# One merged stage for prompt attention and paged sample attention in a forgetting-attention layer

## The reference, cut to what matters

```python
# prompt: blocks of 128 queries, c_k = cumulative sum of log forget values
sc = einsum('bqhd,bkhd->bhqk', qi, k) * scale + ci[..., None] - c_k[:, :, None, :]
sc = where(pi[:, None] >= pos[None, :], sc, NEG_INF)
out = einsum('bhqk,bkhd->bqhd', softmax(sc), v)

# sample: 2048 past keys of a sequence lie in 16 pages of 128 keys of a pool
k_past, v_past, lf_past = (pool[page_table] ... for k, v and log forget values)
r_past = cumsum(lf_past, axis=1, reverse=True) - lf_past
s_past = einsum('bqhd,bkhd->bhqk', q, k_past) * scale + cq + r_past
s_new  = einsum('bqhd,bkhd->bhqk', q, k) * scale + cq - cq', causal
p = softmax(concatenate([s_past, s_new], axis=-1))
out = einsum(p past, v_past) + einsum(p new, v)
```

## Time and profile before

| what | value |
|---|---|
| runs of the kernel | 2106.39 and 2113.93 us, median 2110.16 us |
| the profiled execution | span 2106.6 us |
| PE busy | 1840.3 us (87%) |
| PEld busy | 1610.9 us (76%) |
| DVE busy | 982.8 us (47%) |
| ACT busy | 537.1 us (25%) |
| POOL busy | 172.2 us (8%) |
| forget sums, prompt and sample stages of layer 1 | from 1106.40 to 1595.12 us |

### The profile page before, as it was taken

The page is one execution under the profiler, slowest core; times in us unless marked ns, Lnnn a source line. Parts: engine busy times, 40 slices in busy tenths (PEclk is TensorE's granted clock), DMA queues, the critical chain, the costliest instruction groups (busy, mean ns, idle before and its releaser), DMA issues.

```text
span 2106.6 us, 36927 instructions
## 1 busy us (share of the span) xinstructions
PE 1840.3 (87%) x13959; PEld 1610.9 (76%) x13959; DVE 982.8 (47%) x1689; ACT 537.1 (25%) x880; POOL 172.2 (8%) x332
## 2 busy tenths in 40 slices
PE   5999466899999999799766788888878899999998
PEld 4876345799999999699634456566557799999997
DVE  5396965533333222776457864444433533333222
ACT  3210233322222111433222323222312322222110
POOL 1010000000000000444100001122220000000000
PEclk9999867999999999999878769999988999999999
DMA  3210121222222322223421027788873222223221
GB/s 113 63 38 30 40 76 61 59 80 85 84 80 81 95 83 71 64 75 87 159 91 61 1 84 276 283 290 312 302 231 97 60 80 86 83 80 91 83 82 58
DMA packets 231243, 224.30 MB, mean 106 GB/s; under 512 B 12114, under 2 KB 199588, under 8 KB 231162
## 3 DMA queue, kind: packets, MB, share of 16 engines
q1 hardware_dynamic: 210736, 150.49, 23.1%
q0 software_dynamic: 19008, 69.43, 9.5%
q10 hardware_dynamic: 1418, 3.29, 0.5%
HBM read 215.37 MB, written 7.80 MB: 106 GB/s over the span
## 4 chain that ended last, share of the span: by engine, by line
PE 74%; DVE 14%; ACT 4%; DMA 3%; issue 3%; POOLq 0%; ACTq 0%; DVEq 0%; POOL 0%
PE ps L1335 54%; PE ps L1708 5%; PE ps L1544 3%; DMA vring<-in_cache_fox_v_dram 3%; PE ps L1720 2%; PE ps L1317 2%; PE ps L1746 2%; DVE tmp L382 1%; DVE stat L468 1%; PE ps L1725 1%; ACT prob L1046 1%; DVE prob L459 1%; DVE prob L494 1%; DVE yc L687 1%; DVE aL L386 1%
## 5 line engine op out<-in xcount | busy, mean ns | idle before, releaser
L1335 PE MATMUL ps<-aH,wH 128*128 128x288 f32 x2224 | 487.5, 301 | 51.8 <-DVE aL L386 34.6
L1335 PE MATMUL ps<-aL,wH 128*128 128x288 f32 x2224 | 480.3, 298 | 0.0
L1335 PE MATMUL ps<-aH,wL 128*128 128x288 f32 x2224 | 479.9, 298 | 0.0
L1335 PEld LDWEIGHTS ps<-aH,wH 128*128 128x128 f32 x2224 | 361.9, 191 | 61.2 <-issue 39.1
L363 DVE TENSOR_TENSOR wL<-raw,wH 128x1024 fp32r<-128x1024 f32 (+1 forms) x179 | 232.0, 1296 | 337.0 <-ACT wH L985 333.9
L1335 PEld LDWEIGHTS ps<-aL,wH 128*128 128x128 f32 x2224 | 362.3, 191 | 0.0
L1335 PEld LDWEIGHTS ps<-aH,wL 128*128 128x128 f32 x2224 | 362.2, 191 | 0.0
L985 ACT ACTIVATE wH<-raw 128x1024 fp32r<-128x1024 f32 (+1 forms) x179 | 198.8, 1111 | 386.6 <-PE ps L1335 358.1
L1335 PE MATMUL ps<-gH,wH 128*128 128x288 f32 x704 | 151.1, 296 | 4.8 <-DVE gL L605 4.8
L1335 PE MATMUL ps<-gH,wL 128*128 128x288 f32 x704 | 151.1, 295 | 0.0
L1335 PE MATMUL ps<-gL,wH 128*128 128x288 f32 x704 | 150.9, 295 | 0.0
(11 more groups left out here) (295 smaller groups left out, 1982.8 us busy)
## 6 DMA issues: line engine op xcount, KB each, us to landing
kring<-in_cache_fox_k_dram SPq DMA_DIRECT2D x128, 384.0 KB, 4.7
vring<-in_cache_fox_v_dram POOLq DMA_DIRECT2D x128, 384.0 KB, 5.2
raw<-in_w_gate_up_dram SPq DMA_DIRECT2D x88, 512.0 KB, 3.8
raw<-in_w_down_dram SPq DMA_DIRECT2D x32, 704.0 KB, 4.6
raw<-in_fox_w_in_dram SPq DMA_DIRECT2D x21, 512.0 KB, 3.9
raw<-in_w_out_dram SPq DMA_DIRECT2D x16, 512.0 KB, 3.8
raw<-in_conv_w_in_dram SPq DMA_DIRECT2D x14, 512.0 KB, 3.9
raw<-in_w_mem_kv_dram SPq DMA_DIRECT2D x8, 512.0 KB, 3.4
```

Of the source, the lines that this page charges most:

```text
L1335: mm = nc.tensor.matmul(ps[:, 2 * slot + h, 0:HT], weights[:, w], a[:, k0 + k, h * HT:(h + 1) * HT], start=(first and k == 0 and weights i ...
```

## The change

The forget sums move beside the memory attention: `forget(i)` runs in its unit i. The prompt and sample stages become one. It has SLOTS = 32 slots, SPB = 4 for each sequence, of SPG = 4 pages (512 keys), and four more slots for the values of the last sequence. The loops over b are gone; every slot is written out. The rings have three chunks.

*Prompt.* `fox_step` cuts the prompt into STEPS = 30 steps of up to 512 key columns of one head (two heads or blocks together where blocks are short), five for two heads. Step i has its maximum, exponential and scaling in slot i, its transposes and values in slot i + 1; its scores stand at the end of slot i - 1.

*Keys.* `keys_T` transposes keys on DVE in 32 by 32 blocks from SBUF to SBUF, two instructions of 128 x 1536 in a slot, into `KT[s % 2]`. The queries are laid out to match: `qr` is built by 16 ACT copies ahead of `memory_kv(1)`, and `spread(b)` makes `qx4` and `qx` from it and from `qkT` by eight ACT copies.

*Scores.* `slot_scores` makes 96 products of tiles with 32 rows and 32 columns (128 keys), and 48 that add `rx` (32 keys). The scores of a sequence stay in PSUM banks 0 to 3 until its exponential has read them; the copies to `S` go.

*Values.* At the head of a slot PE multiplies both chunks of values that fall to the slot, for the sequence before, ahead of the slot's scores. Bank 4 holds their sum, bank 5 the scores of a prompt step, and banks 6 and 7 are taken in turn (`turn_ready`, `turn_free`) by probability transposes, prompt values, new scores, outputs and broadcast forget sums (`c_keys`).

*Other engines.* ACT makes the copies from PSUM that DVE made (probabilities, `ncb`, the scaled output). POOL copies `rx` for four pages (`forget_rows`) into a single buffer, for which it waits until the scores before have been made (`sc_done`); the copy for slot 5 + j stands in its program ahead of the load of chunk 2j + 3. SP waits for `kt_done` where it waited for `kt_ready`.

In the diff below DVE's part comes first, then ACT's, PE's, SP's and POOL's.

```diff
-    RING = 4
+    RING = 3
+    SLOTS = NB * NCH // 2
+    SPB = SLOTS // NB
+    SPG = 2 * CPG
...
+    STEPS = 5 * HP
...
+    def fox_step(i):
+        two, k = divmod(i, 5)
+        e, hp = two % 2, two - two % 2
+        parts = ([(0, 3, 0, SEQ)], [(1, 3, 0, SEQ)], [(0, 0, 0, P), (0, 2, P, 3 * P)], [(1, 0, 0, P), (1, 2, P, 3 * P)],
+                 [(0, 1, 0, 2 * P), (1, 1, 2 * P, 2 * P)])[k]
+        return k, e, [(n, hp + n, t, col, keys) for n, t, col, keys in parts]
...
+            def forget(i):
+                if i == 0:
+                    dve.wait_ge(lf_in, 16 * NB * NP)
+                    nc.vector.tensor_reduce(lftot[:], lfrow[:].rearrange("n (k h) -> n h k", h=NH), AX_X, ALU.add).then_inc(lftot_done, 1)
+                if i < 2 * (NH // 4):
+                    g = i % (NH // 4)
+                    bank = group()
+                    nc.vector.tensor_copy((lfT if i < NH // 4 else rtok)[:, 4 * g:4 * g + 4, :].rearrange("p h n -> p (h n)"),
+                                          bank).then_inc(tr_free, 1)
+            attend(u, MEM_UNITS, mb1, len(MEM_UNITS), forget)
...
+            def keys_T(s):
+                if s >= 2:
+                    dve.wait_ge(sc_done, s - 1)
+                for x in range(2):
+                    n = 2 * s + x
+                    dve.wait_ge(k_in[n % RING], 32 * (n // RING + 1))
+                    nc.vector.transpose(KT[s % 2][:, CPG * x:CPG * x + CPG, :].rearrange("p a n -> p (a n)"),
+                                        kring[n % RING][:].rearrange("p a n -> p (a n)")).then_inc(kt_done, 1)
...
+            def step_top(i):
...
+                if k == 0:
+                    for n in range(2):
+                        wait_taken(dve, ("ncb", i // 5, n))
+                dve.wait_ge(f_scores, i + 1)
+                for n, hp, t, col, keys in parts:
+                    last = nc.vector.scalar_tensor_tensor(out=pr[:, col:col + keys], in0=ps[:, 5, col:col + keys],
+                                                          scalar=ctok[:, t, 2 * hp + e:2 * hp + e + 1], in1=ncb[:, n, 0:keys],
+                                                          op0=ALU.add, op1=ALU.add)
+                link(last)
+                if k < 2:
...
+                for x, (n, hp, t, col, keys) in enumerate(parts):
+                    last = nc.vector.tensor_reduce(st[:, x:x + 1], pr[:, col:col + keys], AX_X, ALU.max, negate=True)
+                last.then_inc(f_max, 1)
...
+            def sample_top(b):
...
+                link(nc.vector.tensor_reduce(stat[0:ROWS, 55:56], S[:, NPAST:NPAST + NS], AX_X, ALU.max, negate=True))
+                dve.wait_ge(sc_done, SPB * (b + 1))
+                link(nc.vector.tensor_reduce(stat[0:ROWS, 54:55], ps[0:ROWS, 0:4, :].rearrange("p a n -> p (a n)"), AX_X, ALU.max, negate=True))
+                link(nc.vector.scalar_tensor_tensor(out=stat[0:ROWS, 56:57], in0=stat[0:ROWS, 54:55], scalar=stat[0:ROWS, 55:56],
...
+            for s in range(SLOTS + SPB):
+                b, cc = divmod(s, SPB)
+                if cc == 0 and b:
+                    sample_top(b - 1)
+                    if s <= STEPS:
+                        step_lo(s - 1)
+                if s < STEPS:
+                    step_top(s)
+                if s + 1 < SLOTS:
+                    keys_T(s + 1)
+                if s < STEPS:
+                    step_sums(s)
+                if cc == 0 and b:
+                    sample_sum(b - 1)
+                elif 1 <= s <= STEPS:
+                    step_lo(s - 1)
...
+            act.wait_ge(hn_done, Z + 1 + HP)
+            act.wait_ge(mL_done, KD)
+            for e in range(2):
+                for c in range(2):
+                    r = slice(DH * e + DQ * c, DH * e + DQ * c + DQ)
+                    for a in range(4):
+                        last = nc.scalar.activation(qr[DQ * a:DQ * a + DQ].rearrange("p (g e) c n -> p g e c n", e=2)[:, :, e, c, :],
+                                                    qkT[r, 0:HP, SEQ:T], ACT.Copy)
...
+            def spread(b):
+                if b:
+                    act.wait_ge(sc_done, SPB * b)
+                    wait_turn(act, ("new", b - 1))
+                for m in range(4):
...
+            def sample_exp(b):
+                act.wait_ge(smax_done, b + 1)
+                nc.scalar.activation(S[:, 0:NPAST].rearrange("p (g a i) -> p a g i", a=4, i=DQ),
+                                     ps[0:ROWS, 0:4, :].rearrange("p a (g i) -> p a g i", i=DQ), ACT.Exp, bias=stat[0:ROWS, 56:57],
+                                     accum_out=stat[0:ROWS, 57:58])
...
+            for s in range(SLOTS + SPB):
+                b, cc = divmod(s, SPB)
+                if 1 <= s <= STEPS:
+                    step_probT(s - 1)
+                if cc == 0 and b:
+                    if b >= 2:
+                        sample_scale(b - 2)
+                    if b < NB:
+                        spread(b)
+                    if s <= STEPS:
+                        step_hi(s - 1)
+                    sample_exp(b - 1)
+                if s < STEPS:
+                    step_exp(s)
+                if cc == 1 and b >= 2:
+                    sample_hi(b - 2)
+                if not (cc == 0 and b) and 1 <= s <= STEPS:
+                    step_hi(s - 1)
+                if s < STEPS:
+                    step_scale(s)
+                if (s + 1) % 5 == 0 and s + 1 < STEPS:
...
+            def step_scores(i):
+                k, e, parts = fox_step(i)
+                if i:
+                    pe.wait_ge(f_max, i)
+                r = slice(DH * e, DH * e + DH)
+                for n, hp, t, col, keys in parts:
+                    mm = nc.tensor.matmul(ps[:, 5, col:col + keys], qkT[r, hp, t * P:(t + 1) * P], qkT[r, HP + hp, 0:keys], start=True, stop=True)
+                mm.then_inc(f_scores, 1)
...
+            def slot_scores(s):
+                b, cc = divmod(s, SPB)
+                pe.wait_ge(kt_done, 2 * s + 2)
+                if cc == 0:
+                    pe.wait_ge(qx_done, b + 1)
+                    if b:
+                        pe.wait_ge(sexp_done, b)
+                k4 = KT[s % 2]
+                def out(a, j):
+                    return ps[QR * j:QR * j + QR, a, cc * P:(cc + 1) * P]
+                for m in range(4):
+                    for c in range(2):
+                        for a in range(4):
+                            for j in range(3):
+                                blk, r = 2 * (4 * j + m) + c, slice(DQ * a, DQ * a + DQ)
+                                nc.tensor.matmul(out(a, j).rearrange("p (g i) -> p g i", g=SPG), qx4[r, blk, :], k4[r, :, blk * DQ:blk * DQ + DQ],
+                                                 start=(m == 0 and c == 0), stop=False, skip_group_check=True, tile_position=(DQ * a, QR * j))
+                pe.wait_ge(rx_done, s + 1)
+                for g in range(SPG):
+                    for a in range(4):
+                        for j in range(3):
+                            r = slice(DQ * a, DQ * a + DQ)
+                            mm = nc.tensor.matmul(out(a, j)[:, g * DQ:(g + 1) * DQ], rx[r, g, 4 * j:4 * j + 4, :].rearrange("p h q -> p (h q)"),
+                                                  ident[r, DQ * a:DQ * a + DQ], start=False, stop=(g == SPG - 1), skip_group_check=True,
+                                                  tile_position=(DQ * a, QR * j))
+                mm.then_inc(sc_done, 1)
...
+            def values(b, c):
+                n = NCH * b + c
+                pe.wait_ge(v_in[n % RING], 32 * (n // RING + 1))
                 if c == 0:
...
+            c_keys(0)
+            step_scores(0)
+            for s in range(SLOTS + SPB):
+                b, cc = divmod(s, SPB)
+                step = 1 <= s <= STEPS
+                if step:
+                    step_probT(s - 1)
+                if cc == 0 and b:
+                    if step:
+                        step_values(s - 1)
+                    sample_probT(b - 1)
+                if b:
+                    values(b - 1, 2 * cc)
+                    values(b - 1, 2 * cc + 1)
+                if s < SLOTS:
+                    slot_scores(s)
+                    if cc == SPB - 1:
+                        new_scores(b)
+                if cc == 1 and b >= 2:
+                    sample_out(b - 2)
+                if not (cc == 0 and b) and step:
+                    step_values(s - 1)
+                if (s + 1) % 5 == 0 and s + 1 < STEPS:
+                    c_keys((s + 1) // 5)
+                if s + 1 < STEPS:
+                    step_scores(s + 1)
...
+                which = [sp.value_load(pages[0:1, CPG * n + pp:CPG * n + pp + 1], min_val=0, max_val=N_PHYS - 1) for pp in range(CPG)]
+                if n >= RING:
+                    sp.wait_ge(kt_done, n - RING + 1)
                 for pp in range(CPG):
...
+            def forget_rows(s):
+                if s:
+                    pool.wait_ge(sc_done, s)
```

(87 more changed lines are left out.)

541 lines of the change are left out of this document (230 added, 311 removed).

## The result

The changed kernel takes 2228.98 us (runs 2219.03 and 2238.93) against 2110.16: a ratio of 1.0555, interval 1.049 to 1.0621. It is slower, where 2083 was forecast, and outside the range of 2012 to 2155.

A forecast was written before the change was run, and what follows sets the result against it. The prediction took a ring of waits through POOL's value pages to bound most new slots; 9 + 27 + 254 + 134 + 37 = 461 us in place of 488.7 gave a median of 2083 us, range 2012 to 2155.

The forecast's parts named there:

- the scores of a slot: PE's score and rx products in each slot: 1.73 us, 0.67 at 7 ns a tile start, 0.2 to drain; 2.6 us.
- the rival of separate tiles: Score products on four row groups go one after the other: 5.2 us more in 32 slots, 2249 us; chance 0.10.
- forget sums beside the memory attention: Forget sums moved into the memory stage, where PE waits for DVE and ACT, hide in part: 9 us, ends 5 and 13.
- first four slots: Slots without value products go at DVE's pace, 6.3 us each after a start: 27 us (22 to 40).
- 21 slots within a sequence: Slots set by the closed ring from scores through rx copy and value pages: 12.1 us each, 254 us.
- 7 slots at a head: Slots at a sequence's start, through exponential, probability transposes, values and scores: 19.2 us each (17 to 22), 134 us.
- tail: Four last slots without scores, with remaining values and the output: 37 us (34 to 42).
- The ring of waits: Scores, rx copy, two value pages issued, landed, multiplied, scores: 10.6 us, 12.1 with the clock, a slot; chance 0.52.
- Everything else of a slot lies in the shadow: A slot's other PE work, 4.4 to 6 us, hides between scores and landing of values, 7.05 us.
- The clock: PE's granted clock in the new slots is taken as 0.7, so 3.6 us of PE work take 5.1.
- The transposes: DVE's key transposes from SBUF to SBUF: 1.94 us for 1536 columns, two in a slot 3.9.
- DVE against POOL: DVE's transposes keep POOL from issuing value pages: 40 to 82 us in all, 2123 to 2165; chance 0.09.

The follow-up runs named there:

- e1: Changed kernel with the rx products of a page cut from twelve to three and three quarters of the forget sums left out: 2153.19 us.
- e2: Changed kernel with the rx products issued a second time with a block of zeros: 2321.75 us.
- e3: Changed kernel with POOL's value loads put ahead of the waiting rx copy: 2233.35 us.
- e5: Changed kernel with forget sums transposed by DVE, 12 products adding them in place of 48, and no rx copy by POOL: 2108.72 us.
- e8: Changed kernel with scores for two slots at once, sums transposed by DVE, and values of odd slots behind the scores: 2060.69 us.
- the pairs: Changed kernel with scores made once for two slots, 256 keys to a product, and sums transposed by DVE: 2094.99 us.
- e12: Changed kernel with only the first three chunks of values loaded and multiplied again and again: 2168.36 us.
- e11: Changed kernel with 192 long-met waits added to PE's program behind the scores of each slot: 2540.05 us.

## Why the prediction was wrong

The step that failed is the scores of a slot: 2.6 us, with "the start of a tile, some 7 ns" as what sets the pace. The pace inside a burst was near what the sum gives at the clock of 0.7 that it takes elsewhere: 185 of a slot's 192 score passes begin between 1214.66 and 1217.02, 2.4 us, so the four row groups do overlap, and the rival of separate tiles falls. What the step left out is that the products and their weight loads have to come in at all: 576 instructions, where the scores of four pages took 144 before, key transposes included (768 products of each of three lines over 64 chunks, each with its weight load; two of the lines are in the earlier trace rows, the third is here).

```profile
L1725 PE MATMUL ps<-ident,rx 128*32 128x128 f32 x768 | 39.6, 275 | 0.0
```

Scores and sums took 5.0 to 9.4 us a slot, 6.8 in the mean over the 28 slots with values: 2.7 of stops, and 4.0 without them (2.6 is 3.7 at a clock of 0.7). e1 and e2 show the effect of the count by taking instructions away and adding them. That the kernel before ran most of its sample stage from a loop, and the changed kernel has every slot written out, is a second difference, which the prediction priced at nothing as well. No run puts the slots in a loop, so the two are not told apart.

| step | predicted | measured |
|---|---|---|
| forget sums beside the memory attention | 9 | 9.8 (1116.2 against 1106.4) |
| first four slots | 27 | 50, with 16 of stops |
| 21 slots within a sequence | 254, 12.1 each | 336, 16.0 each |
| 7 slots at a head | 134, 19.2 each | 173, 24.7 each |
| tail | 37 | 37.4 |

The sum is 606 us in place of 461, 145 more; the stops are 96 us. As e3 shows, a stop can stand where another wait would, so the 96 are not a price by themselves. The cause of the other 49 stays open. The runs show that they tend to go with the stops: where these are fewer, the clock is mostly higher (0.66 at 149 us, 0.68 at 96, 0.74 at 50, 0.84 at 33, but 0.81 at 16).

*The ring of waits* was there in each of its parts: the `rx` copy 0.51 us (0.48), pages issued 1.14 apart (1.23), landing 4.1 (4.0).

```profile
1206.43 0.51 POOL L2191 COPY rx<-rtok 128x384 f32<-128x384 f32 x1 [10.08 <-PE ps L1884]
1207.58 0.54 POOL L2206 DMA_DIRECT2D vring<-in_cache_fox_v_dram  x1 [0.64 <-issue]
1208.72 0.54 POOL L2206 DMA_DIRECT2D vring<-in_cache_fox_v_dram  x1 [0.60 <-issue]
```

But it was not what set the time: PE waited 35 us for values in all (12 before, in the stretch of the earlier trace rows), and with 8 us of it left (e3) the time was the same. "Everything else of a slot lies in the shadow" was costed at full clock, 4.4 to 6 us; at 0.7, the clock that the ring was given in the same paragraph, it is 6.3 to 8.6, and the shadow was 7.05. That this is why two slots of three don't wait for values is argued, not shown.

*The clock* of 0.7 came out as 0.69, with stops in it that the prediction didn't have; with fewer of them it was 0.81 (e5) and 0.84 (e8). So the match is luck. *The transposes* took 1.75 us for 1.94. The estimate from the Trainium skill (VectorE: DVE Perf Modes, "The three transpose paths"), 3.7 us, is not what this trace shows. One of 128 x 128 in float32 by itself took 0.31 us in e5, so twelve times a small one was the wrong way to reckon. *DVE against POOL*: 12 value pages were issued while a transpose ran, 25 in e8, each in 0.54 us as the others. The Trainium skill (SBUF — State Buffer, the "DVE blocks DMA" trap) says that POOL can't write descriptors while DVE runs an operation in a two-port mode, as a float32 copy from SBUF to SBUF does; it doesn't name transposes, and with these no such hold shows.

## What to carry to other kernels

Count the instructions of a stage, not only its columns: PE's small tiles overlap well here, but 256 instructions that ran in 1.7 us came in 3.8 us after the boundary before, in the median, and 5.2 in e3, where the values were asked for earlier. Before a stage is written out in small products, look for the form with fewer and wider ones (e5 and e8 took the same sums from 1.056 to 1.002 and 0.981). Where a loop is written out, its instructions have to come in each time; compare the instruction queue's row with PE's count before and after. A wait that the chain names can be where another resource catches up; taking it away (e3) may only show that one.

## What the runs showed of the hardware

The instruction queue's packets on the page follow the written-out program's length to the packet: 18 fewer, 24 more, 45 fewer than 122 for 144 x 32 and 192 x 32 instructions and for the pairs (360 x 32), 256 to a packet. A pause of PE at such a boundary ended 1.2 to 1.5 us after its packet had been moved. When the packet begins depends on other transfers (1.4 us after the boundary before in e12, 2.7 in e3). A wait on PE that has long been met cost 0.10 us in e11. Transposes of 32 x 32 blocks by DVE in float32 run at 1.14 ns a column (1752 ns for 1536).
